# Leftover rows of an expert pair: 128 half rows and four transposes in place of 64 whole rows and eight

## The reference

```python
xn = rmsnorm(h, norm_ffn_g)
scores = sigmoid(xn @ w_router)
_, top_idx = top_k(scores + router_bias, 8)
gates = top_s / sum(top_s) * 2.5          # top_s: the scores of the chosen
y = (silu(xb @ w_gate_e[e]) * (xb @ w_up_e[e])) @ w_down_e[e]    # xb: rows of xn routed to expert e
h = h + routed + shared(xn)               # routed: the sum of gate * y over a token's 8 experts
out = rmsnorm(h, norm_final_g)[:, 16:]
```

## Time and profile before

| | before |
|---|---|
| median of 3 runs | 1817.78 us (1817.76 to 1818.12) |
| profiled execution | 1817.95 us |
| its span, first to last instruction | 1816.2 us |
| TensorE matmuls busy | 1686.2 us, 93% of the span |
| TensorE weight loads busy | 1336.2 us, 74% |
| VectorE, ScalarE, GpSimd busy | 737.5, 632.8 and 644.0 us (41%, 35%, 35%) |
| mean granted TensorE clock | 0.965 |
| DMA | 348.68 MB, 192 GB/s over the span |

### The profile page before, as it was taken

One profiled execution on the slowest core, in us unless ns is written; L12 is line 12 of the kernel. 1 busy time (PEld: TensorE's weight loads), 2 busy tenths in 40 slices (PEclk: granted clock), 3 DMA queues, 4 the chain that ended last, 5 costly groups with the idle time before them and its releaser, 6 DMA issues. The chain is left out here.

```text
span 1816.2 us, 29882 instructions
## 1 busy us (share of the span) xinstructions
PE 1686.2 (93%) x10076; PEld 1336.2 (74%) x10076; DVE 737.5 (41%) x1532; ACT 632.8 (35%) x1004; POOL 644.0 (35%) x790
## 2 busy tenths in 40 slices
PE   4989899999998899997999999999999999999981
PEld 3767655655554356675999999999999999999970
DVE  5010266666665676541333333333333333333332
ACT  7111233333333332111434433444344334443433
POOL 1200000025552122331544554445455444554540
PEclk9989899999999899998999999999999999999995
DMA  4011100010006101143999999999999999999986
GB/s 141 1 47 35 35 24 23 23 34 24 23 12 250 65 24 48 47 163 131 305 319 322 318 322 312 323 325 313 318 316 317 327 310 323 328 310 320 321 259 222
DMA packets 111949, 348.68 MB, mean 192 GB/s; under 512 B 14591, under 2 KB 48064, under 8 KB 94510
## 3 DMA queue, kind: packets, MB, share of 16 engines
q1 hardware_dynamic: 78094, 260.23, 39.7%
q0 software_dynamic: 33824, 88.06, 20.0%
HBM read 290.46 MB, written 57.79 MB: 192 GB/s over the span
## 5 line engine op out<-in xcount | busy, mean ns | idle before, releaser
L1530 PE MATMUL gu<-XS,place 128*128 128x160 f32 x4224 | 597.1, 300 | 0.7 <-ACT XS L1609 0.7
L1530 PEld LDWEIGHTS gu<-XS,place 128*128 128x128 f32 x4224 | 584.3, 190 | 6.2 <-ACT XS L1609 1.1
L1665 DVE TENSOR_TENSOR WL<-place,WH 128x2048 fp32r<-128x2048 f32 x66 | 152.1, 2305 | 339.0 <-ACT WH L1601 339.0
L469 PE MATMUL bank<-xT,wi 128*128 128x512 f32 x512 | 241.6, 613 | 0.0
L1614 ACT ACTIVATE SS<-gu 128x160 f32<-128x160 f32 x132 | 40.2, 304 | 372.3 <-PE gu L1530 372.3
L469 PEld LDWEIGHTS bank<-xT,wi 128*128 128x128 f32 x512 | 93.5, 194 | 90.4 <-issue 90.4
L1670 DVE TENSOR_TENSOR SS<-SS,gu 128x160 f32<-128x160 f32 x132 | 41.7, 316 | 261.1 <-ACT SS L1614 261.1
L357 POOL TENSOR_TENSOR place<-place 128x514 f32<-128x514 f32 (+1 forms) x8 | 12.0, 1494 | 371.5 <-ACT place L539 371.2
L1435 POOL COPY gta<-tables 128x1 f32 (+1 forms) x66 | 130.4, 1977 | 11.7 <-POOLq L781 11.7
L1624 ACT ACTIVATE YE<-ype,gta 128x512 f32<-128x512 f32 x132 | 91.0, 690 | 112.4 <-PE ype L1554 112.4
L940 POOL DMA_INDIRECT slot_table<-pay,si x64 | 63.2, 988 | 183.7 <-DVEq L1238 166.7
(11 more groups left out here) (279 smaller groups left out, 2506.0 us busy)
## 6 DMA issues: line engine op xcount, KB each, us to landing
place<-in_w_gate_e SPq DMA_DIRECT2D x67, 1024.0 KB
place<-in_w_up_e SPq DMA_DIRECT2D x67, 1024.0 KB
place<-in_w_down_e SPq DMA_DIRECT2D x66, 1024.0 KB
wi<-in_w_in SPq DMA_DIRECT2D x16, 512.0 KB, 3.9
xn_rows<-place SPq DMA_DIRECT2D x9, 512.0 KB, 2.6
xt<-in_x SPq DMA_DIRECT2D x8, 512.0 KB, 5.7
wbuf<-in_w_in SPq DMA_DIRECT2D x8, 512.0 KB, 4.1
wo<-in_w_out SPq DMA_DIRECT2D x2, 2048.0 KB, 10.2
```

The costliest lines, as they stand in the source:

```text
L469: last = pe.matmul(bank[blk][:, :], wbuf[s][:, t, :], K.xT[:, t, cols], start=(t == 0), stop=(t == KT - 1))
L1530: last = pe.matmul(gu[f][:, k, :], raw[:, t, f * P:f * P + P], XS[:, q, t, :], start=(t == 0), stop=(t == KT - 1))
L1665: tt(WL[q][:, :], WR[q][2][:, :], WH[q][:, :].bitcast(F32), ALU.subtract).then_inc(s_dlo, 1)
```

## The change

The leftover rows of a pair come as 128 half rows. xn2_rows is read as twice as many rows of 512 values, K.rest holds 2 * row + h for the half h, in 128 partitions: the first 64 get the left halves of the 64 rows, the other 64 the right halves. XR is 128x512, full, and four transposes turn it: columns 0 to 63 of a result belong to block t, columns 64 to 127 to block t + 4. The second copy of keep_rest reads these from the same bank. The clearing of the lower half of XR (L947) goes, with its semaphore.

For that, a half row must hold whole blocks. So normed writes its values in the order "(t k)" in place of "(k t)": X2 and the stored rows have block t in 128 neighbouring columns, and every transpose of such rows (turn, turned) reads neighbouring columns. The index column is made by a matmul of twice as many columns (tbq has each entry twice) and a product and sum with side, 0 in the first 64 partitions and 1 in the others.

```diff
-    K.rest = K.tab[0:2 * CAP1, 4 * ITEMS:4 * ITEMS + PAIRS].bitcast(I32)
+    K.rest = K.tab[:, 4 * ITEMS:4 * ITEMS + PAIRS].bitcast(I32)
...
-            pool.memset(K.slot[2][2 * CAP1:, :], 0.0).then_inc(s_xr, 1)
...
-            pool.indirect_dma_start(K.slot[2][0:2 * CAP1, :], None, xn2_d, bass.IndirectOffsetOnAxis(ap=K.rest[:, 0:1], axis=0)) \
+            pool.indirect_dma_start(K.slot[2][:, 0:D // 2], None, xn2_d.rearrange("r (h n) -> (r h) n", h=2), bass.IndirectOffsetOnAxis(ap=K.rest[:, 0:1], axis=0)) \
...
-                rows = X2[j % 2].rearrange("p (k t) -> p t k", t=KT)
+                rows = X2[j % 2].rearrange("p (t k) -> p t k", t=KT)
...
-            pe.matmul(ms[1][0:2 * CAP1, 0, 0:PAIRS], tbq[:, :, :].rearrange("i q c -> i (q c)"), pairsel[:, :],
+            pe.matmul(ms[1][:, 0, 0:PAIRS], tbq[:, :, :, :].rearrange("i h q c -> i (h q c)"), pairsel[:, :],
...
-                stt(X2[j % 2], H[j % NH], sh[:, TT + j:TT + j + 1], gffn[:, :], ALU.mult, ALU.mult).then_inc(s_x2, 1)
+                by_k = [a.rearrange("p (k t) -> p k t", t=KT) for a in (H[j % NH], gffn[:, :])]
+                stt(X2[j % 2].rearrange("p (t k) -> p k t", t=KT), by_k[0], sh[:, TT + j:TT + j + 1], by_k[1], ALU.mult, ALU.mult) \
+                    .then_inc(s_x2, 1)
...
+            for h in range(2):
+                step(nc.vector.memset(side[h * 2 * CAP1:(h + 1) * 2 * CAP1, :], float(h)))
...
-                ts(tbq[:, q, :], tbl[:, P:CAP, 0], par[:, q:q + 1], None, ALU.mult).then_inc(s_tx, 1)
+                ts(tbq[:, :, q, :], tbl[:, P:CAP, 0].rearrange("i (o c) -> i o c", o=1).to_broadcast([ITEMS, 2, CAP1]),
+                   par[:, q:q + 1], None, ALU.mult).then_inc(s_tx, 1)
...
-            nc.vector.tensor_copy(K.rest, ms[1][0:2 * CAP1, 0, 0:PAIRS])
+            ts(K.rest, ms[1][:, 0, 0:PAIRS], 2.0, side[:, 0:1], ALU.mult, ALU.add)
...
-                pool.indirect_dma_start(XR[0:2 * CAP1, :], None, xn2_d, bass.IndirectOffsetOnAxis(ap=gj[:, :], axis=0)) \
+                pool.indirect_dma_start(XR, None, halves_d, bass.IndirectOffsetOnAxis(ap=gj[:, :], axis=0)) \
...
-                rows = XG[q][:, :].rearrange("p (k t) -> p t k", t=KT)
+                rows = XG[q][:, :].rearrange("p (t k) -> p t k", t=KT)
...
-                rows = XR[:, :].rearrange("p (k t) -> p t k", t=KT)
-                for t in range(KT):
-                    last = pe.transpose(xp[t // 4][:, t % 4, :], rows[:, t, :], K.ident[:, :])
+                for t in range(KT // 2):
+                    last = pe.transpose(xp[0][:, t, :], XR[:, t * P:t * P + P], K.ident[:, :])
...
-                         xp[h][:, :, 0:2 * CAP1].rearrange("p t (q s) -> p q t s", q=2)).then_inc(s_rk, 1)
+                         xp[0][:, :, 2 * CAP1 * h:2 * CAP1 * (h + 1)].rearrange("p t (q s) -> p q t s", q=2)).then_inc(s_rk, 1)
```

More of the change, by code:

```diff
@@ L814, in phase_out_route @@
         par = sb("par", [ITEMS, 2])
-        quarter, lowi, rowc, pidx = (sb(n, [P, 1]) for n in ("quarter", "lowi", "rowc", "pidx"))
+        quarter, side, lowi, rowc, pidx = (sb(n, [P, 1]) for n in ("quarter", "side", "lowi", "rowc", "pidx"))
         rowi = sb("rowi", [ITEMS, 1], I32)
@@ L821, in phase_out_route @@
         tbx = late[0:ITEMS, 320:320 + 2 * P].rearrange("i (k a c) -> i k a c", k=2, c=CAP1)
-        tbq = late[0:ITEMS, 640:640 + 2 * CAP1].rearrange("i (q c) -> i q c", q=2)
+        tbq = late[0:ITEMS, 640:640 + 4 * CAP1].rearrange("i (h q c) -> i h q c", h=2, q=2)
         cnt, ext, inc, le, zero = (late[:, 768 + k * E_N:768 + (k + 1) * E_N] for k in range(5))
@@ L837, in phase_out_route @@
         s_k0, s_k = sem("patterns_cleared"), sem("patterns_set")
-        s_sig, s_ag, s_xr, s_ix = sem("sigmoids"), sem("slots_written"), sem("rest_cleared"), sem("indices_ready")
+        s_sig, s_ag, s_ix = sem("sigmoids"), sem("slots_written"), sem("indices_ready")
         s_sq, s_ms, s_rt = sem("squares"), sem("mean_squares"), sem("roots")
@@ L950, in _ @@
                 .then_inc(K.s_g[0], 16)
-            pool.wait_ge(s_xr, 1)
-            pool.indirect_dma_start(K.slot[2][0:2 * CAP1, :], None, xn2_d, bass.IndirectOffsetOnAxis(ap=K.rest[:, 0:1], axis=0)) \
+            pool.indirect_dma_start(K.slot[2][:, 0:D // 2], None, xn2_d.rearrange("r (h n) -> (r h) n", h=2), bass.IndirectOffsetOnAxis(ap=K.rest[:, 0:1], axis=0)) \
                 .then_inc(K.s_gr, 16)
@@ L1344, in phase_experts @@
         WL = [sb(f"WL{i}", [P, KT * FF], F32R) for i in two]
-        XG, XR = K.slot[0:2], K.slot[2]
+        XG, XR = K.slot[0:2], K.slot[2][:, 0:D // 2]
         XS = sb("XS", [P, 2, KT, CAP])
@@ L1353, in phase_experts @@
         gi = [sb(f"gi{i}", [P, 1], I32) for i in two]
-        gj = sb("gj", [2 * CAP1, 1], I32)
+        gj = sb("gj", [P, 1], I32)
         si = [(sb(f"sia{i}", [P, 1], I32), sb(f"sib{i}", [P, 1], I32)) for i in two]
         gt = [(sb(f"gta{i}", [P, 1]), sb(f"gtb{i}", [P, 1])) for i in two]
+        halves_d = xn2_d.rearrange("r (h n) -> (r h) n", h=2)
         acc_q = acc_d.rearrange("r (j n) -> (r j) n", j=QUARTERS)
```

## The result

| | before | after |
|---|---|---|
| median of four runs each | 1817.77 us | 1801.28 us (1798.54 to 1802.79) |
| ratio, 95% interval | | 0.9900 [0.9886, 0.9915] |
| profiled execution | 1817.95 us | 1802.62 us |
| its span | 1816.2 us | 1800.8 us |
| TensorE matmuls busy | 1686.2 us | 1674.0 us |

The changed kernel is 1% faster. Its median is 1.7 us under the forecast and inside the range of 1801 to 1811 us. The ratio is the better measure, since it compares runs of one chip: 0.9900 of 1817.77 us is 1799.6 us (1797.1 to 1802.3), 18.2 us less than before where the sum had 14.9. By it the range began 1.4 us too high, though the interval reaches into it. The changed kernel was timed twice more, each time beside the kernel before, with ratios of 0.9892 [0.9876, 0.9907] and 0.9917 [0.9903, 0.9930]: three estimates of the gain, of 15.1, 18.2 and 19.6 us.

What follows compares the result with a forecast made beforehand. TensorE's stream was taken to bound the routed experts' loop. Loop transposes -14.6, first group -0.7 and small operations +0.4 gave -14.9 us, so 1803 us (-0.8%), range 1801 to 1811 with chance 0.81.

Steps and rivals of the forecast that it cites:

- The loop's term: Routed experts' loop and its last turns: four fewer transposes in each of 32 groups, 0.455 us a pair, -14.6 us.
- the strided writes: Route phase: eight normed writes with values 512 bytes apart, taken as 0 from a decay-factor product using every other column.
- The other end: Loop's transposes: smaller gain if sequencer work between groups stays behind, 32 x 0.285 = -9.1 us.
- The first group: Leftover transposes ahead of the loop, at the lower clock: four fewer, -0.7 us.
- Contiguous transposes, nothing: All 66 groups of ordinary transposes: reading 128 neighbouring columns instead of every eighth gains nothing, 188 against 192 ns.
- the dear bound: Normed writes priced by a predicated copy of 0.73 us: factor 1.7, +0.9 us on each of eight, +7.2 at most.
- visibly in two of eight turns: Strided-writes rival, route phase: TensorE waits for VectorE there, so between 2 and 8 x 0.9 us; 1805 to 1810, chance 0.08.
- either is hidden while TensorE sets the pace: Rest gathers in the loop: GpSimd's own part and up to 0.47 us a pair of DMA time add nothing.
- The +0.4 for small operations: Route phase: rest column, two tbq products and two memsets of side, 0 to +0.5 us, taken as +0.4.
- The DMA engines took over: Rival: DMA engines hold the pair at 27.95 us, 1814, chance 0.11; if extra packets also cost time, 1829, chance 0.05.
- the bound of 0.47 us a pair: Rest gathers: 64 more packets at 0.117 us each over 16 DMA engines cost at most 0.47 us a pair.
- The accumulation chain: Rival on GpSimd: later landings of adding DMAs lose half the gain, 1810, chance 0.07; sign: sia waits in all 66 turns.

Runs made afterwards that it cites:

- The change alone: The kernel before with only four of the eight transposes of leftover rows made, rows, gathers and column order unchanged: 1802.39 us, ratio 0.9916.
- the order alone: The kernel before with only the column order changed to "(t k)", whole leftover rows and eight transposes kept: 1818.82 us, ratio 0.9995.
- its repetition: The changed kernel run again with no edit: 1798.22 us, ratio 0.9892.
- where the reads step: The changed kernel with normed writing neighbouring columns and reading both inputs at a step of eight columns: 1801.47 us, ratio 0.9907.
- without the two products: Two of down's three products left out, in the kernel before (1745.86 us) and in the changed kernel (1714.54 us).

## Why the prediction was right or wrong

The loop's term was right. What failed is the rest of the sum: it had no term for what the new gathers change outside the loop (the drain, -3.8 us, and the way to the first transposes, about -1.2), and it took 0 for the strided writes, which cost +1.1 to +2.6. The two errors partly cancel, and that the plain median fell inside the range is luck.

**The transposes, right.** The sum had -14.6 us from 32 groups of four at 0.114 us. The change alone gave 14.9, the changed kernel's loop 14.1. The other end, -9.1 with sequencer gaps that stay, is excluded: the even turn fell by 0.44 us. The first group was sized 0.7 and measured 0.86.

**Contiguous transposes, nothing, right for a poor reason.** 188 against 192 ns was the wrong comparison, since the contiguous load of these rows lasts 142 ns. But start to start the group of eight is the same, 0.901 and 0.900 us. What moves the loop by up to 1.5 us between kernels with equal transposes is mostly down, whose twelve loads take 2.629 us with the order alone, 2.636 with the transposes alone, 2.644 before and 2.651 in the changed kernel and its repetition. Twice a pair, 32 pairs: 0.015 us are 1 us, which is the changed kernel's 0.8 us against the transposes alone. Its cause is open.

**The strided writes, a step that failed.** "I take 0", by the row of the product at a step of two columns. The Trainium skill's lines of 16 bytes ("SBUF — State Buffer", Specifications (TRN2)), which the prediction named, pointed the right way, and by them the row couldn't speak on it: two fp32 values 8 bytes apart still share a line. The price is +0.73 us on each of eight, near the dear bound of 0.9. What of that reaches the end was well bounded by the rival, "visibly in two of eight turns". The windows from one normed write to the next, kernel before, first three and one later:

```profile
598.24:615.15 16.91, 13.37 (x44) 7.24 (x44) 12.92 (x16) 7.84 (x13) 0.00 (x0) 0.80 0.08 31
615.15:639.07 23.92, 20.23 (x62) 10.41 (x62) 18.23 (x48) 8.02 (x14) 8.30 (x8) 0.93 0.06 23
639.07:662.87 23.80, 21.28 (x73) 11.56 (x74) 18.10 (x47) 8.03 (x14) 7.72 (x8) 0.93 0.06 23
...
688.59:717.73 29.14, 29.14 (x139) 18.61 (x138) 20.00 (x50) 8.40 (x15) 8.23 (x8) 1.00 0.17 55
```

and the changed kernel, in the profile of its repetition:

```profile
596.85:613.77 16.92, 13.38 (x44) 7.25 (x44) 13.53 (x17) 7.84 (x13) 0.00 (x0) 0.80 0.08 31
613.77:638.25 24.48, 20.10 (x62) 10.51 (x62) 18.92 (x48) 8.01 (x14) 8.30 (x8) 0.93 0.06 22
638.25:664.08 25.83, 22.83 (x73) 12.41 (x74) 18.59 (x47) 8.03 (x14) 8.29 (x8) 0.87 0.06 21
...
689.78:718.92 29.14, 29.14 (x139) 18.57 (x138) 20.58 (x50) 8.40 (x15) 8.22 (x8) 1.00 0.17 55
```

From the fourth tile on TensorE has no gap, and 0.6 us more work of VectorE costs nothing. In the second and third, TensorE's idle time (length less PE busy) grows from 3.69 to 4.38 and from 2.52 to 3.00 us. From the first write to the eighth it is 9.7 us in all five profiles with contiguous writes, 10.9 in the six with stepped writes and 11.2 where the reads step. In the third stretch there can be a second price: TensorE is busy 1.5 us longer at a granted clock of 0.87 in place of 0.93. Four of the seven with a step had it (the whole stretch is then 178.1 to 178.3 us, else 176.7 to 176.8), none of the five without (175.5 to 175.7). That the longer waits bring the lower clock about is likely by this count, not shown. So the writes cost 1.1 or 2.6 us, not 0 and not the 5.8 that a count of operations gives.

**The drain, the step that was missing.** The prediction followed the gathers as far as the DMA engines and GpSimd's own part in the loop ("either is hidden while TensorE sets the pace") and put nothing for them elsewhere. Between the experts and phase_final nothing hides them. All five profiles with 64 rows in the rest gather have a drain of 5.17 us, all nine with 128 have 1.41. What the engine does in that time stays open. Nor was the way to the first transposes looked at: from the first gather to the first main-row transpose the five need 14.2 to 15.2 us and the nine 12.5 to 14.1, about 1.2 us less on average. Why is not shown either.

**The new sum.** -14.1 (loop) - 0.9 (first group) - 3.8 (drain) - 1.2 (first gather) + 1.1 to 2.6 (writes) is -18.9 to -17.4 us, and the three ratios give -18.2, -19.6 and -15.1. The terms of the start and the end were found after the result, so the sum describes these runs and doesn't test itself. The +0.4 for small operations was too much: the rest column took 0.27 us in place of 0.20 and the two tbq products 0.248 each in place of 0.235, 0.1 us in all.

**The rivals.** The DMA engines took over in neither form. TensorE had no wait in the loop, and the bound of 0.47 us a pair was for 64 packets more, which don't exist, since two half rows travel as one. The limit of about 358 GB/s that the prediction took from the Trainium skill ("DMA: Bandwidth & Descriptors", Specifications) is no ceiling for this core: over 100 us of the loop without the two products the changed kernel moved 363 GB/s, and in phase_final 414 to 426 GB/s in slices of 1.4 us. The accumulation chain: sia waited for the DMA 44 times in place of 35 over the whole span, on the way to the 66 that were named as the sign, but TensorE kept its pace, and from the end of the loop to the last adding DMA it was 16.5 to 20 us in full kernels of either kind. This rival got a chance of 0.07 and the DMA engines 0.16, and it is the chain that comes next: it held the pair at 25.6 and 24.7 us once TensorE had less to do.

**The noise.** "This kernel's runs agree to 0.02%" came from three runs. In later ones, on three chips, the kernel before spread over 11.5 us, over 5.5 to 8.3 on any one. Between profiles, the stretch before the route phase, the same code in all, took from 559 to 564 us. A range with a low end 1.8 us under the forecast claimed more than one term's size could carry.

## What to carry to other kernels

Price a transpose or matmul group by the difference of two neighbouring turns, start to start. That was right to 0.01 us, while the durations of single loads, 142 and 188 ns for the same pace, say little. A row that is to stand for a stepped access must have the same step: 2, 4 and 8 columns each behave in their own way, on VectorE and on TensorE. And follow a change of a DMA's shape to the places where its engine drains, and count idle time of the engine that sets the pace, not operations, for what of a dearer one is paid. To learn what would limit a loop next, take work from the engine that sets the pace and look which queue then waits for nothing but itself, before naming bandwidth.

## What the runs showed of the hardware

- GpSimd's DRAIN behind a block with rest gathers of 64 rows into 64 partitions took 5.17 us, behind one with 128 rows into 128 partitions 1.41 us, whatever the row size (2 or 4 KB) and with or without the memset. Why is open. Only the rest gather's shape was varied, and no kernel had other counts than 64 and 128.
- The DMA engines' share was 1.00 to 1.03 at 305 to 342 GB/s, and 1.04 at 355 GB/s over 120 us in which TensorE still had no gap. No run shows a limit of theirs. Over the loop without the two products they moved 348 GB/s with rest gathers into 64 partitions and 360 with 128, held back by a chain of adding DMAs that wait for each other's landing, 9.7 and 9.2 us after the issue.
- VectorE's product of 128x1024 fp32: 1.285 us contiguous, 2.01 with writes 512 bytes apart, 2.08 with reads 32 bytes apart, 1.50 as two operations of runs of 16 bytes. The Trainium skill's lines of 16 bytes ("SBUF — State Buffer", Specifications (TRN2)) fit all four.
- TensorE's fp32 load of 128x128: 142 ns at no step, 188 at a step of eight columns, 208 at four; eight of them to the next matmuls 0.900, 0.901 and 0.967 us.
- In four of the seven executions in which two waits of TensorE were together 1.2 to 1.4 us longer, the stretch behind them had a granted clock of 0.87 in place of 0.93 and took another 1.5 us; in none of the five without.
